# Reading the stationary tiles of an f32r kernel with a step of two words

## The reference

```
def swiglu(h, w_gate, w_up, w_down):
    return (silu(h @ w_gate) * (h @ w_up)) @ w_down          # 2048 -> 5632 -> 2048

hs = concat([meta, x])
hs = hs + 0.5 * swiglu(rmsnorm(hs, ffn1_norm), ffn1_w_gate, ffn1_w_up, ffn1_w_down)
hs = hs + token_mixing(rmsnorm(hs, mix_norm), w_in, b_in, ..., w_out)
hs = hs + 0.5 * swiglu(rmsnorm(hs, ffn2_norm), ffn2_w_gate, ffn2_w_up, ffn2_w_down)
return rmsnorm(hs, final_norm)[:, 16:]

# token_mixing: u = h @ w_in + b_in, cut into five parts of 1024 channels: b, c, v, a, g
# y_sc = b * causal_conv(c * v, 3 taps); z = causal_conv(a * sigmoid(g), 31 taps) + bias
# y_cf = silu(layernorm(z)); return concat([y_sc, y_cf]) @ w_out
```

## Time and profile before

| | |
|---|---|
| median of 3 runs | 1904.35 us (1903.69 to 1904.44) |
| the profiled execution | 1904.94 us, its span 1902.9 us, granted clock 0.998 |
| TensorE, products | 12639, busy 1878.2 us (99%) |
| TensorE, loads of stationary tiles | 12639, busy 1751.7 us (92%) |
| VectorE | 1212 instructions, busy 1121.6 us (59%) |
| ScalarE | 1176 instructions, busy 922.6 us (48%) |
| DMA | 342.21 MB, mean 180 GB/s |

### The profile page before, as it was taken

One profiled execution on the slowest core, in us unless ns is written; L12 is line 12 of the kernel. 1 busy time (PEld: TensorE's weight loads), 2 busy tenths in 40 slices (PEclk: granted clock), 3 DMA queues, 4 the chain that ended last, 5 costly groups with the idle time before them and its releaser, 6 DMA issues.

```text
span 1902.9 us, 31295 instructions
## 1 busy us (share of the span) xinstructions
PE 1878.2 (99%) x12639; PEld 1751.7 (92%) x12639; DVE 1121.6 (59%) x1212; ACT 922.6 (48%) x1176; POOL 22.2 (1%) x33
## 2 busy tenths in 40 slices
PE   8999999999999999999999999999999999999997
PEld 7999999999999999999998788888888888888886
DVE  6555555555554544468898998555566555544443
ACT  6434433443443444359888665444444444433443
POOL 4000000000000000000000000000000000000000
PEclk9999999999999999999999999999999999999999
DMA  6655555555555565555655566666656666666663
GB/s 196 189 176 176 170 173 176 172 172 175 176 171 174 177 174 172 175 175 169 186 182 168 163 191 191 193 187 188 188 176 187 188 196 189 212 187 187 189 189 121
DMA packets 283387, 342.21 MB, mean 180 GB/s; under 512 B 10656, under 2 KB 223746, under 8 KB 283169
## 3 DMA queue, kind: packets, MB, share of 16 engines
q1 hardware_dynamic: 282960, 340.83, 58.7%
q0 software_dynamic: 288, 0.19, 0.0%
q10 hardware_dynamic: 64, 0.14, 0.0%
HBM read 339.02 MB, written 2.10 MB: 179 GB/s over the span
## 4 chain that ended last, share of the span: by engine, by line
PE 96%; DVE 2%; ACT 1%; DMA 0%; issue 0%; ACTq 0%; DVEq 0%
PE ps L451 20%; PE ps L446 17%; PE ps L444 17%; PE ps L445 17%; PE ps L452 10%; PE ps L547 4%; PE ps L545 4%; PE ps L546 4%; DVE w_lo L806 1%; PE ps L404 0%; PE ps L555 0%; DMA m_tok<-in_meta_tokens 0%; DVE res L939 0%; DVE ln_sum L1003 0%; DVE res L932 0%; DVE y_f L921 0%
## 5 line engine op out<-in xcount | busy, mean ns | idle before, releaser
L806 DVE TENSOR_TENSOR w_lo<-raw,w_hi 128x1024 fp32r<-128x1024 f32 x640 | 784.4, 1227 | 660.7 <-ACT w_hi L609 658.9
L609 ACT ACTIVATE w_hi<-raw 128x1024 fp32r<-128x1024 f32 x640 | 676.5, 1059 | 862.7 <-PE ps L446 493.2
L444 PE MATMUL ps<-x_both,w_hi 128*128 128x272 f32 (+1 forms) x1920 | 555.2, 289 | 0.0
L446 PE MATMUL ps<-x_both,w_lo 128*128 128x272 f32 (+1 forms) x1920 | 554.3, 289 | 0.0
L445 PE MATMUL ps<-x_both,w_hi 128*128 128x272 f32 (+1 forms) x1920 | 551.8, 287 | 0.0
L451 PE MATMUL ps<-x_both,w_hi 128*128 128x512 f32 x1536 | 537.0, 393 | 0.5 <-DVE w_lo L806 0.5
L452 PE MATMUL ps<-x_both,w_lo 128*128 128x256 f32 x1536 | 430.9, 281 | 0.0
L445 PEld LDWEIGHTS ps<-x_both,w_hi 128*128 128x128 f32 x1920 | 362.6, 189 | 0.1
L444 PEld LDWEIGHTS ps<-x_both,w_hi 128*128 128x128 f32 x1920 | 361.9, 188 | 0.1
L446 PEld LDWEIGHTS ps<-x_both,w_lo 128*128 128x128 f32 x1920 | 361.8, 188 | 0.0
L451 PEld LDWEIGHTS ps<-x_both,w_hi 128*128 128x128 f32 x1536 | 288.3, 188 | 66.6 <-DVE w_lo L806 0.9
(11 more groups left out here) (129 smaller groups left out, 1074.2 us busy)
## 6 DMA issues: line engine op xcount, KB each, us to landing
raw<-in_ffn_w_gate SPq DMA_DIRECT2D x176, 512.0 KB, 3.7
raw<-in_ffn_w_up SPq DMA_DIRECT2D x176, 512.0 KB, 3.6
raw<-in_ffn_w_down SPq DMA_DIRECT2D x176, 512.0 KB, 3.8
raw<-in_w_in SPq DMA_DIRECT2D x80, 512.0 KB, 3.5
raw<-in_w_out SPq DMA_DIRECT2D x32, 512.0 KB, 4.7
x_tok<-in_x SPq DMA_DIRECT2D x4, 512.0 KB, 9.5
out_y<-o_tok SPq DMA_DIRECT2D x8, 256.0 KB, 3.6
gain_tok<-in_final_norm SPq DMA_DIRECT2D x1, 1024.0 KB, 4.6
```

The source lines that it names most:

```text
L444: pe.matmul(dst, w_high, act_high, start=first, stop=False)
L446: return pe.matmul(dst, w_low, act_high, start=False, stop=last)
L609: act.activation(w_hi[s][:, :], raw[s][:, :], ACT.Copy).then_inc(hi_ready, 1)
L806: dve.tensor_tensor(w_lo[s][:, :], raw[s][:, :], w_hi[s][:, :].bitcast(F32), ALU.subtract).then_inc(lo_ready, 1)
```

## The change

The high and low parts of a block share one buffer of 2048 words. For all stages but second down they are interleaved word by word (high, low, high, low), so that a stationary tile's 128 words per partition lie two apart; for second down, where the weights stream, they lie one behind the other as before. In second down the stationary operand is `a2_both`, and there the high and low activations are interleaved instead. ScalarE and VectorE write and read the same views. The instructions, their order, their waits and the DMAs are the same.

```
--- before.py
+++ after.py
@@ -95,8 +95,14 @@
 
 
         raw = [sb(f"raw{i}", [P, BLOCK]) for i in range(RING)]
-        w_hi = [sb(f"w_hi{i}", [P, BLOCK], F32R) for i in range(RING)]
-        w_lo = [sb(f"w_lo{i}", [P, BLOCK], F32R) for i in range(RING)]
+        w_both = [sb(f"w_both{i}", [P, 2 * BLOCK], F32R) for i in range(RING)]
+        w_columns = [w[:, :].rearrange("p (n b) -> p b n", b=2) for w in w_both]
+        w_rows = [w[:, :].rearrange("p (b n) -> p b n", b=2) for w in w_both]
+
+        def w_parts(phase, s):
+
+            both = w_rows[s] if phase == "down2" else w_columns[s]
+            return both[:, 0, :], both[:, 1, :]
         res = sb("res", [P, KD, T])
         t12 = sb("t12", [P, 4, T])
         t1, t2 = t12[:, 0:2, :], t12[:, 2:4, :]
@@ -122,9 +128,9 @@
         gain_tok = at("gain_tok", x_at + 4 * HALVES * D, [P, D])
         sq_tok = at("sq_tok", x_at + 4 * (HALVES + 1) * D, [P, HALVES, BANK])
         a_both = at("a_both", a_at, [P, 2, KF, T], F32R)
-        a2_both = at("a2_both", a_at, [P, 2, KF, SEQ], F32R)
+        a2_both = at("a2_both", a_at, [P, KF, SEQ, 2], F32R)
         a_of = {"gu1": (a_both[:, 0, :, :], a_both[:, 1, :, :]),
-                "gu2": (a2_both[:, 0, :, :], a2_both[:, 1, :, :])}
+                "gu2": (a2_both[:, :, :, 0], a2_both[:, :, :, 1])}
 
         gu2_lo = at("gu2_lo", a_at + 4 * 2 * KF * SEQ, [P, SET, SEQ])
         assert SET * SEQ <= 2 * KF * (T - SEQ)
@@ -487,11 +493,11 @@
                                 cols = slice(c * 256 + j * P, c * 256 + (j + 1) * P)
                                 bank = SET * parity + 2 * (i % 2) + j
                                 if phase == "gu2":
-                                    m = wide_product(bank, w_hi[s][:, cols], w_lo[s][:, cols],
+                                    m = wide_product(bank, *(w[:, cols] for w in w_parts(phase, s)),
                                                      x_both[:, :, k, toks], x_hi[:, k, toks],
                                                      k == 0, k == KD - 1)
                                 else:
-                                    m = product(bank, width[phase], w_hi[s][:, cols], w_lo[s][:, cols],
+                                    m = product(bank, width[phase], *(w[:, cols] for w in w_parts(phase, s)),
                                                 x_hi[:, k, toks], x_lo[:, k, toks], k == 0, k == KD - 1)
                         m.then_inc(block_used, 1)
                         if norm and first_group and i == (6 if norm == "start" else 3):
@@ -515,11 +521,11 @@
                             k = 2 * i + c
                             cols = slice(c * 512 + j * P, c * 512 + (j + 1) * P)
                             if phase == "down1":
-                                m = product(SET * parity + j, width[phase], w_hi[s][:, cols], w_lo[s][:, cols],
+                                m = product(SET * parity + j, width[phase], *(w[:, cols] for w in w_parts(phase, s)),
                                             high[:, first_k + k, toks], low[:, first_k + k, toks],
                                             k == 0, k == n_k - 1)
                             else:
-                                m = wide_product(SET * parity + j, w_hi[s][:, cols], w_lo[s][:, cols],
+                                m = wide_product(SET * parity + j, *(w[:, cols] for w in w_parts(phase, s)),
                                                  both[:, :, first_k + k, toks], high[:, first_k + k, toks],
                                                  k == 0, k == n_k - 1)
                     m.then_inc(block_used, 1)
@@ -540,7 +546,7 @@
                         dst = ps[:, HALVES * g + h, :]
                         for c in range(2):
                             k = 2 * i + c
-                            w_high, w_low = (w[s][:, c * BANK:(c + 1) * BANK] for w in (w_hi, w_lo))
+                            w_high, w_low = (w[:, c * BANK:(c + 1) * BANK] for w in w_parts("down2", s))
                             a_hi, a_lo = a_of["gu2"]
                             pe.matmul(dst, a_hi[:, k, toks], w_high, start=k == 0, stop=False)
                             pe.matmul(dst, a_lo[:, k, toks], w_high, start=False, stop=False)
@@ -606,7 +612,7 @@
                 ahead = before_block(phase, g, i)
                 if not isinstance(ahead, int) or ahead >= RING:
                     act.wait_ge(block_used, ahead - (RING - 1))
-                act.activation(w_hi[s][:, :], raw[s][:, :], ACT.Copy).then_inc(hi_ready, 1)
+                act.activation(w_parts(phase, s)[0], raw[s][:, :], ACT.Copy).then_inc(hi_ready, 1)
 
             def operand(phase, norm, t):
 
@@ -803,7 +809,8 @@
             def low(phase, g, i):
                 s = slot(phase, g, i)
                 dve.wait_ge(hi_ready, before_block(phase, g, i) + 1)
-                dve.tensor_tensor(w_lo[s][:, :], raw[s][:, :], w_hi[s][:, :].bitcast(F32),
+                w_high, w_low = w_parts(phase, s)
+                dve.tensor_tensor(w_low, raw[s][:, :], w_high.bitcast(F32),
                                   ALU.subtract).then_inc(lo_ready, 1)
 
             def operand(phase, norm, t):
```

6 lines of the change are left out of this document (3 added, 3 removed).

## The result

The changed kernel takes 1916.8 us (median; 1916.7 to 1917.7) against 1904.1 for the one before, a ratio of 1.0068 with a 95% interval of 1.005 to 1.0085: slower by 0.7%, where 1784 us were forecast.

What follows compares the result with a forecast made beforehand. TensorE was taken as the bound, with VectorE the bound from 860 to 1009 and 1055 to 1107 us. 1904.9 us less 128.2 of exposed load time, plus 7 given back, gave 1784 us; range 1765 to 1940.

Steps and rivals of the forecast that it cites:

- the stake of 167 us: All product stages: time left behind products in which nothing streams, 167 us of 1902.9.
- rows 8: Second down's f32 residual additions, 128 columns, follow each other in 111 ns, so a hidden load needs at most 111.
- case (a): All products: strided loads run behind the stream, leaving 2.5 ns; 128.2 us saved, 7 given back, 1784 us; chance 0.47.
- rows 7: Sums of squares: loads cost 2 to 3 ns behind half-rate f32 streams, but an f32 load behind full rate 13.
- Case (b): All products: nothing changes, the 13 ns are a tile change or fixed hold, the stride is free; 1905 us; chance 0.25.
- (d): From 860 us: no load gain, VectorE's subtraction 0.67 us dearer each, TensorE waits for w_lo; 1937 us; chance 0.14.
- the 7 us given back: From 860 to 1055 us: half of TensorE's 14 us gain lost, as VectorE has 173.1 us of work there.
- (c): All products: the load holds the stream for twice 13.3 ns; 166 us more, 2070 us; chance 0.14.
- I take nothing: Weight blocks: ScalarE's and VectorE's accesses with a step of two words cost nothing over 1059 and 1227 ns.

Runs made afterwards that it cites:

- m1_alone: TensorE alone, no layer computed: 40 series of 48 products varying step, columns and type; at 512 columns 227 ns at step 1, 233 at step 2.
- e7: Kernel before, no step, one 32-byte tile allocated ahead so the weight buffers begin 32 bytes further on: 1906.69 us, ratio 1.0012.
- e8: Changed kernel with its steps of two words, its weight buffers 32 bytes further on: 1929.43 us, ratio 1.0132.
- m3_place: TensorE alone, 35 series at 512 columns with tile or moving operand shifted: 226.7 to 234.4 ns at step 1, 230.0 to 235.6 at step 2.
- m2_sweep: TensorE alone, 44 series sweeping tile columns, streamed columns, place and type: a tile of 8 columns takes 226.7 ns at 512 streamed, step 1.
- e9_both32: Kernel before, no step, weight buffers and second gate-up's activations both 32 bytes further on: 1899.71 us, ratio 0.9977.

## Why the prediction was wrong, point by point

**What bounds the kernel** was right: TensorE, in time that lies between the products; the stake of 167 us is real, in the sense that bfloat16 products leave 2.5 ns where f32r ones leave 13 (m1_alone).

**The step that failed** is the reading of that remainder as the load's: "the load seems to take four words at a time and to hold the stream for that long". The 13.3 ns are as long as 32 cycles, 32 is a quarter of 128 columns, and from this equality I made a mechanism. A tile of 8 columns leaves the same 13.3 ns, and tiles between leave more, so the number isn't a quarter of the tile's columns. And the load doesn't take four words at a time: where it sets the pace it needs 111.7 ns for 128 columns, the 111 of rows 8 that the prediction took for its floor. The Trainium skill has, in TensorE: Matmul & The Clock Gate, section LDWEIGHTS (loading the stationary operand), the columns over 1.2 as its ns, by which an estimate is 107; the trace is 5 ns above. The load was hidden all along. So case (a), 128 us of saving, had nothing to give. The 2.5 ns of rows 7 belong to products that aren't f32r: f32 at half rate leaves 2.5 (229.2 over 226.7), bfloat16 at full rate 2.5 as well. The text had the row that speaks against (a), the f32 load that pays 13 ns behind a full-rate stream, named it, and gave (a) 0.47 all the same.

**Case (b) came nearest**, a remainder that stays and moves with the addresses, and its size: "other addresses could shift this case by some 10 us either way" stood against a measured +12.7. Its "the stride is free" is borne out in second down at one place (e7 and e8), not in second gate-up, where the step cost 7 us at both. I gave the shift a twentieth on either side. It should have been most of (b), since the individual spacings of 120 to 130 ns showed the dependence and this layout changes where every word lies; and more of it on the slow side, because the 227 ns of second down, equal for every product, were the best case and had one way to go.

**The range.** 1916.8 lies inside 1765 to 1940, by luck: the upper end was there for (d), whose mechanism didn't occur, and (b) with its shift reached to 1915. Two ends of (a) were also summed wrongly. Without the 7 us given back and with 109.2 ns for 256 columns the lower one is 1773, not 1765; the terms of the upper one give 1830, not 1835. Neither matters for the outcome.

**The rule on the fast load**, which (b) took from the Trainium skill (TensorE: Matmul & The Clock Gate, the section on weight-path perf modes), led to the right side for a reason that the runs don't bear out in f32r. By the rule the fast load is on at any column step from -1,023 to 1,024; here the pace of the load goes from 111.7 to 117.8, 173 and 233 ns at steps of 1, 2, 3 and 4 words, so f32r loads show no such mode. The bfloat16 series (216 ns at steps of 1, 2 and 4 elements, the last 8 bytes) only say that their loads are no longer than the stream. That makes (c), too, a wrong picture with its own price of 166 us: the load's pace does get slower with the step, by 6.1 ns of 111.7, and that stays hidden behind 256 columns (120.0 ns at either step) and more.

**ScalarE and VectorE.** "I take nothing" was right for VectorE (1229 against 1227 ns) and for the path. ScalarE's copy with a strided output is 90 ns longer, 9% (1148 against 1058), which I had at zero; from 860 to 1009 us it is busy 133.6 of 149 us, so it stays covered. Case (d) didn't occur. The Trainium skill's rule on SBUF lines (Advanced Engine Details and Errata, SBUF Cachelines) holds for VectorE at 8 bytes, and nearly for loads, which go from 118 ns at a step of 8 bytes (L120) to 173 at 12 and 233 at 16 (L104); ScalarE's 9% it doesn't tell.

**The moving operands** were right to stay contiguous: at a step of two words they take 453 ns instead of 227, which the rule on lines doesn't tell either.

What stays open: why an f32r product leaves 10 to 21 ns at all; by which rule the place acts, and what besides it made one and the same series take 226.7 and 231.7 ns; why the interleaving costs 2 us more in second down than the shifts did; and whether second gate-up has any place at which the step doesn't cost its 7 us (two were tried; with TensorE alone the step gained 3 ns a pair).

## What to carry to other kernels

A remainder that equals a neat number of cycles is no evidence of where it comes from: vary the one quantity that the explanation names (here the tile's columns) in a series of products of its own before building on it. Where TensorE is busy all the time and multiplies f32r, the relative place of the stationary tile and the moving operand within 256 bytes was worth some 3% of a product of 512 columns here and comes free: compare any change of layout with a plain shift of its tiles, or the shift is taken for the change. Let stationary tiles have a step if something else wants it (two words cost at most 9 ns a product here), but not moving operands, whose time it doubled.

## What the runs showed of the hardware that was not expected

- The time of an f32r product depends on where its operands lie: 226.7 to 234.4 ns for 512 contiguous columns over twelve places, with nothing else running (m3_place); bfloat16 products gave 215.8 at each step tried (m1_alone, m2_sweep).
- An f32r load has a pace of its own of 111.7 ns for 128 contiguous columns, 118 at a step of two words, 173 at three, 233 at four; the last two are longer than the stream of 256 or 272 columns, and then set the spacing (m1_alone).
- The granted clock fell from 1.00 to 0.50, the lower of its two levels, in the series of m1_alone with 128 columns and a step of three words or more, where TensorE's record is busy without a gap but each product waits for its load; it came back to 1.00 in the next series of 512 columns. By stretch, L118 (step 1) and L124 (step 4):

```profile
174.00:179.60 5.60, 5.60 (x51) 5.60 (x51) 0.00 (x0) 0.00 (x0) 0.00 (x0) 1.00 0.00 0
195.00:206.00 11.00, 11.00 (x49) 11.00 (x48) 0.00 (x0) 0.00 (x0) 0.00 (x0) 0.50 0.00 0
```

- Weight buffers and activations 32 bytes further on, with no other change, gave 0.23% (e9_both32, interval 0.14 to 0.32%); a shift together with the step cost 1.3% (e8_step_shift32).
